# One pick in three beside attention added by VectorE, the first rotations moved into the projection's stage, and 64 candidate places for a head instead of 256

## The reference, cut to what matters

```python
sc = einsum('thpc,hpnc->thpn', q, sub_keys)            # 8 heads, 2 halves, 128 keys
v_half, i_half = lax.top_k(sc, 16)
cand = (v_half[:, :, 0, :, None] + v_half[:, :, 1, None, :]).reshape(t, 8, -1)   # 16 x 16
top_s, pos = lax.top_k(cand, 16)
expert = take_along_axis(cand_idx, pos, -1)            # 8 x 16 = 128 rows for a token
g = softmax(top_s)
act = gelu(einsum('thkd,td->thk', u_tab[expert], xc))
out = einsum('thk,thkd->td', g * act, v_tab[expert])
```

## Time and profile before

| | us |
|---|---|
| median of 3 runs | 2328.1 |
| the profiled execution: its own time | 2328.23 |
| its span | 2326.5 |
| PE busy | 1780.1 (77%) |
| DVE busy | 1429.7 (61%) |
| ACT busy | 786.7 (34%) |
| POOL busy | 625.0 (27%) |
| share of q0 (the gathers) in the DMA engines' time | 57.0% |
| chain that ended last: PE, DVE, DMA, ACT | 40%, 21%, 20%, 10% |

### The profile page before, as it was taken

One profiled execution on the slowest core, in us unless ns is written; L12 is line 12 of the kernel. 1 busy time (PEld: TensorE's weight loads), 2 busy tenths in 40 slices (PEclk: granted clock), 3 DMA queues, 4 the chain that ended last, 5 costly groups with the idle time before them and its releaser, 6 DMA issues.

```text
span 2326.5 us, 20848 instructions
## 1 busy us (share of the span) xinstructions
PE 1780.1 (77%) x6626; PEld 1047.3 (45%) x6626; DVE 1429.7 (61%) x2931; ACT 786.7 (34%) x2063; POOL 625.0 (27%) x524
## 2 busy tenths in 40 slices
PE   7587877757867875777787577664888989887987
PEld 3473333522323453332444423553333445566976
DVE  1448864698656479965637986658665234464644
ACT  1211453224334422432442234212564122433532
POOL 0001433444332333533234344425333000000000
PEclk9598989979998888998898898777899999888999
DMA  8068999999999899999989989999999655553542
GB/s 290 16 248 310 415 357 356 420 393 422 407 416 404 336 422 395 423 408 415 386 298 419 368 364 422 408 421 401 346 408 395 239 205 193 196 219 118 182 159 94
DMA packets 108828, 761.55 MB, mean 327 GB/s; under 512 B 13104, under 2 KB 14000, under 8 KB 18608
## 3 DMA queue, kind: packets, MB, share of 16 engines
q0 software_dynamic: 73728, 536.90, 57.0%
q1 hardware_dynamic: 32544, 215.45, 24.3%
q10 hardware_dynamic: 2448, 7.87, 0.9%
HBM read 759.12 MB, written 1.05 MB: 327 GB/s over the span
## 4 chain that ended last, share of the span: by engine, by line
PE 40%; DVE 21%; DMA 20%; ACT 10%; issue 6%; DVEq 1%; POOLq 1%; PEldq 1%; POOL 0%; ACTq 0%; PEld 0%; SPq 0%
DMA sb_work<-in_peer_uv,sb_expert 17%; PE ps_acc L1313 13%; PE bank L439 4%; DVE sb_work L1277 4%; PE bank L1143 3%; DVE sb_x L1285 3%; PE bank L1765 2%; DMA sb_wring<-in_peer_w_q 2%; PE bank L500 2%; PE bank L687 2%; PE ps_acc L1686 2%; ACT L1293 1%; PE bank L502 1%; PE bank L501 1%; ACT sb_probs L740 1%
## 5 line engine op out<-in xcount | busy, mean ns | idle before, releaser
L1313 PE MATMUL ps_acc<-sb_work,sb_diag 128*128 128x512 f32 x1500 | 774.3, 664 | 295.7 <-ACT sb_diag L1302 253.3
L2124 POOL DMA_INDIRECT sb_work<-in_peer_uv,sb_expert x512 | 622.6, 1216 | 1162.1 <-PE ps_acc L1313 587.9
L1277 DVE CUSTOM_DVE_ANT_0 sb_work<-sb_work,sb_h 128x1024 f32<-128x1024 f32 x512 | 620.3, 1223 | 283.7 <-DMA sb_work<-in_peer_uv,sb_expert 267.5
L1313 PEld LDWEIGHTS ps_acc<-sb_work,sb_diag 128*128 128x128 f32 x1500 | 299.7, 211 | 717.8 <-issue 701.0
L1293 ACT ACTIVATE sb_dots<-sb_dots 128x1 f32<-128x1 f32 x512 | 101.7, 199 | 470.7 <-DVE sb_dots L1277 440.8
L1285 DVE SCALAR_TENSOR_TENSOR sb_x<-sb_work,sb_weight,sb_x 128x1024 f32<-128x1024 f32 x137 | 175.5, 1281 | 51.3 <-ACT sb_weight L1294 51.3
L494 DVE TENSOR_TENSOR sb_work_r<-sb_wring,sb_work_r 128x2048 fp32r<-128x2048 f32 (+1 forms) x52 | 109.9, 2126 | 115.2 <-ACT sb_work_r L487 115.2
L439 PE MATMUL bank<-sb_wring,sb_hT 128*128 128x512 f32 (+2 forms) x392 | 158.1, 563 | 24.2 <-DVEq L280 17.4
L1302 ACT ACTIVATE sb_diag<-sb_ident,sb_weight 128x128 f32<-128x128 f32 x375 | 150.6, 401 | 33.0 <-PE ps_acc L1313 21.3
L1294 ACT ACTIVATE sb_weight<-sb_dots,sb_share 128x1 f32<-128x1 f32 x512 | 150.8, 294 | 16.6
L1143 PE MATMUL bank<-sb_hT,sb_wring 128*128 128x128 f32 x1024 | 124.7, 286 | 25.4 <-DMA sb_wring<-in_peer_w_q 22.6
(11 more groups left out here) (294 smaller groups left out, 2125.5 us busy)
## 6 DMA issues: line engine op xcount, KB each, us to landing
sb_wring<-in_w_mix SPq DMA_DIRECT2D x36, 1024.0 KB
sb_wring<-in_peer_w_q SPq DMA_DIRECT2D x32, 1024.0 KB
sb_wring<-in_w_gate SPq DMA_DIRECT2D x32, 1024.0 KB
sb_wring<-in_hyb_w_in SPq DMA_DIRECT2D x20, 1024.0 KB
sb_wring<-in_w_up SPq DMA_DIRECT2D x16, 1024.0 KB
sb_wring<-in_w_down SPq DMA_DIRECT2D x16, 1024.0 KB
sb_wring<-in_mla_w_uq SPq DMA_DIRECT2D x12, 768.0 KB
sb_wring<-in_hyb_w_out SPq DMA_DIRECT2D x8, 1024.0 KB
```

The source lines that it names most:

```text
L1277: e.tensor_tensor_reduce(u, u, h[:, t, :], 1.0, 0.0, ALU.mult, ALU.add, dots[:, i:i + 1]).then_inc(dot_ready, 1)
L1313: last = e.matmul(ps_acc[:, b * 512:(b + 1) * 512], diag[:, number % DIAGS, :], ring[:, n % RING, D + b * 512:D + (b + 1) * 512], start=k ...
L2124: pool.indirect_dma_start(ring[:, n % RING, :], None, a["peer_uv"], bass.IndirectOffsetOnAxis(ap=expert[:, t, n % P:n % P + 1], axis=0)).t ...
```

## The change

There are three edits.

1. The points of `attend` are marked `"both"`, and `share_out` gives a pick that falls on such a point to DVE if its number leaves 2 when divided by 3, and to PE otherwise. So 187 picks are added by DVE, where 137 were.
2. For tile 0, the eight rotations on DVE move from their own stage into the stage of the input projection. Before each, DVE waits until ACT has emptied the last block of columns that the rotation reads.
3. A head's second `top16` runs over 64 places instead of 256. They hold the pairs (row i, column j) of rows 0, 1 to 3, 4 to 7 and 8 to 15 with 16, 8, 4 and 1 columns, among which the 16 largest sums must be. Four smaller additions fill them, and ten more instructions of 128 elements turn a place back into row and column. The weights of the routing's points become smaller (71.5 to 56.5 us in all), so a little more of the picks falls on every other point of the first three feeds.

```diff
-                plan.append(g | value | {"points": [point(6.0), point(6.0)]})
+                plan.append(g | value | {"points": [point(6.0, "both"), point(6.0, "both")]})
...
-            dve_stage(steps)
+            if t:
+                dve_stage(steps)
+            else:
+                project_pe, project_act, _, emptied = project_parts(hT, a["hyb_w_in"], DC, EVEN_COLS, empty_even, "act",
+                                                                    tiles, first)
+                def rotate_behind(e):
+                    first["dve"](e)
+                    e.wait_ge(from_act.sem, sin_v)
+                    for col, rotate_heads in zip((VA, VA, VA, IK, IW, IW, KB, VB), steps):
+                        emptied(e, col)
+                        rotate_heads(e)
+                stage(pe=project_pe, act=project_act, dve=rotate_behind)
...
-            ranked = [point(us) for us in [9.0] + 5 * [6.5] + [3.0] + 6 * [4.5]]
+            ranked = [point(us) for us in [6.0] + 5 * [3.5] + [6.0] + 6 * [4.5]]
...
-                link(e.tensor_tensor(cand, b4[:, :, 0, :].unsqueeze(3).to_broadcast([P, EH, TOP, TOP]),
-                                     b4[:, :, 1, :].unsqueeze(2).to_broadcast([P, EH, TOP, TOP]), ALU.add))
+                for at, i0, ni, nj in ((0, 0, 1, 16), (16, 1, 3, 8), (40, 4, 4, 4), (56, 8, 8, 1)):
+                    link.add(e.tensor_tensor(
...
-                link.add(e.tensor_scalar(pick[0].bitcast(I32), at, 4, None, ALU.arith_shift_right))
-                link(e.tensor_scalar(pick[1].bitcast(I32), at, 15, None, ALU.bitwise_and))
...
+                link(e.tensor_scalar(hi, eighth, -1.0, 0.0, ALU.add, ALU.max))
+                link(e.scalar_tensor_tensor(hi, quarter, -6.0, hi, ALU.add, ALU.max))
+                link(e.scalar_tensor_tensor(hi, place, -48.0, hi, ALU.add, ALU.max))
...
+                link(e.tensor_tensor(lo, place, lo, ALU.subtract))
...
-                    if at is not None and f["filled"][at] == "pe":
+                    filled = None if at is None else f["filled"][at]
+                    if filled == "pe" or filled == "both" and k % 3 == 2:
```

More of the change, by code:

```diff
@@ L403, in project @@
         def project(xT, w, chunks, cols, empty, engine, tiles=range(TILES), first=None):
-            pe, other, points = project_parts(xT, w, chunks, cols, empty, engine, tiles, first)
-            both = {engine: other}
-            if first:
-                both["dve"] = first["dve"]
-            stage(pe=pe, points=points, **both)
+            pe, other, points, _ = project_parts(xT, w, chunks, cols, empty, engine, tiles, first)
+            stage(pe=pe, points=points, **{engine: other})
         def project_parts(xT, w, chunks, cols, empty, engine, tiles, first=None):
@@ L454, in other, with emptied @@
                     p(engine, e)
-            return pe, other, points
+            def emptied(e, col):
+                units = next(units for _, _, bn, c0, units, _ in plan if c0 + bn >= col)
+                units[-1].wait_emptied(e)
+            return pe, other, points, emptied
         places = [work_r[:, 2 * SLOT * i:2 * SLOT * (i + 1)] for i in range(4)] + [work_r[:, 0:SLOT], work_r[:, 3 * SLOT:4 * SLOT]]
@@ L1003, in enter_hybrid @@
             units = [turns.take() for _ in range(2)]
-            project_pe, project_act, _ = project_parts(hT, a["hyb_w_in"], DC, EVEN_COLS, empty_even, "act", [1])
+            project_pe, project_act, _, _ = project_parts(hT, a["hyb_w_in"], DC, EVEN_COLS, empty_even, "act", [1])
             def dve(e):
@@ L1035, in hybrid @@
                 turn_wide(H, hT, DC, tiles)
-                project(hT, a["hyb_w_in"], DC, EVEN_COLS, empty_even, "act", tiles, first)
             steps = []
@@ L1088, in build @@
         pick = [beside[:, 1280:1408], beside[:, 1408:1536]]
+        place, eighth, quarter = (beside[:, 1536 + i * P:1536 + (i + 1) * P] for i in range(3))
         iota16 = sb("iota16", [P, TOP])
@@ L1217, in dve @@
                 rest.pop(0)("dve", e)
[L1219 removed]
+                cf = key_scores.rearrange("p n k -> p (n k)")[:, 0:EH * 64].rearrange("p (h m) -> p h m", h=EH)
                 b4 = best.rearrange("p (h s) k -> p h s k", s=2)
[L1221 to L1222 removed]
@@ L1223, in dve @@
-                cf = key_scores.rearrange("p n k -> p (n k)").rearrange("p (h m) -> p h m", h=EH)
+                for at, i0, ni, nj in ((0, 0, 1, 16), (16, 1, 3, 8), (40, 4, 4, 4), (56, 8, 8, 1)):
+                    link.add(e.tensor_tensor(
+                        cf[:, :, at:at + ni * nj].rearrange("p h (i j) -> p h i j", i=ni),
+                        b4[:, :, 0, i0:i0 + ni].unsqueeze(3).to_broadcast([P, EH, ni, nj]),
+                        b4[:, :, 1, 0:nj].unsqueeze(2).to_broadcast([P, EH, ni, nj]), ALU.add))
@@ L1224, in dve @@
+                link.wait()
                 top16([(cf[:, j, :], top[:, j, :], top_at[:, j, :].bitcast(U32)) for j in range(EH)], [rest.pop(0) for _ in range(5)])
                 at = top_at.rearrange("p n k -> p (n k)").bitcast(I32)
-                link.add(e.tensor_scalar(pick[0].bitcast(I32), at, 4, None, ALU.arith_shift_right))
-                link(e.tensor_scalar(pick[1].bitcast(I32), at, 15, None, ALU.bitwise_and))
-                link.add(e.tensor_copy(hi, pick[0].bitcast(I32)))
-                link(e.tensor_copy(lo, pick[1].bitcast(I32)))
+                link.add(e.tensor_scalar(pick[0].bitcast(I32), at, 3, None, ALU.arith_shift_right))
@@ new lines, in dve @@
+                link.add(e.tensor_scalar(pick[1].bitcast(I32), at, 2, None, ALU.arith_shift_right))
+                link(e.tensor_copy(place, at))
+                link.add(e.tensor_copy(eighth, pick[0].bitcast(I32)))
+                link(e.tensor_copy(quarter, pick[1].bitcast(I32)))
+                link(e.tensor_scalar(hi, eighth, -1.0, 0.0, ALU.add, ALU.max))
+                link(e.scalar_tensor_tensor(hi, quarter, -6.0, hi, ALU.add, ALU.max))
+                link(e.scalar_tensor_tensor(hi, place, -48.0, hi, ALU.add, ALU.max))
@@ L1230, in dve @@
+                link.add(e.tensor_scalar(eighth, hi, 8.0, 8.0, ALU.mult, ALU.add))
+                link(e.tensor_scalar(quarter, hi, 4.0, 24.0, ALU.mult, ALU.add))
+                link(e.scalar_tensor_tensor(lo, hi, 16.0, eighth, ALU.mult, ALU.min))
+                link(e.scalar_tensor_tensor(quarter, hi, 48.0, quarter, ALU.add, ALU.min))
+                link(e.tensor_tensor(lo, lo, quarter, ALU.min))
+                link(e.tensor_tensor(lo, place, lo, ALU.subtract))
                 rest.pop(0)("dve", e)
```

1 line of the change is left out of this document (removed).

## The result

The changed kernel takes 2277.35 us (median of five runs, 2264.04 to 2280.89) where the kernel before takes 2333.31 (five runs). The ratio is 0.9759, 95% interval 0.9727 to 0.9791: 56 us less, between 49 and 64. The forecast was 2282, 46 less than the 2328.1 of then.

The account below looks back on a forecast made before the run. It took stage order as the bound early, then the queues' 421 GB/s ceiling, with attention falling short as POOL waited for PE's picks. Terms 12 + 4 + 5 + 25 = 46 us less than 2328.23 gave 2282 us, range 2254 to 2310.

Parts of the forecast that it names:

- Edit 2 (12 us): Stages before the first gather: tile 0's rotations end with the projection, PE starts transposes at 53.8 instead of 66.04, 12 us less.
- The small extra that the bounds allowed: Behind tile 0's rotations: up to 14 us less instead of 12 if PE, pausing less, keeps its clock.
- The first routing (4 us): First routing: DVE needs 6.4 us less, gathers could start that much earlier; between 2.3 and 6.4, 4 us was taken.
- The lower bound, by bytes: First routing: if bytes decide at once, only (421 - 356)/421 of 15 us comes back, 2.3 us.
- Attention (25 us): Both blocks' attention: two of six picks leave PE, slow groups fall from 19.6 to 16.8 us; 25 us less, bounds 0 to 45.
- the second block's, counted with 4: Second block's attention: its groups were partly at the queues' ceiling already, so 4 of 15.8 us lacking were counted.
- Attention fills to the ceiling: Rival, 20 in 100: attention's queues reach their ceiling, 70 us less in all, 2258 us.
- The clock: PE in attention: with fewer picks a second pick per group may run at 1.2 GHz, costing at most 34 us.
- rival of a cold PE: Rival, 7 in 100: the second cold pick costs 34 us against 28 of relief in attention; 2316 us, about no change.
- They lack 21/421 x 72 = 3.6 us there ... can bring at most these 10.5 us: Three later routings: shorter DVE part and fewer picks bring at most the queues' shortfall, 10.5 us; 5 us was taken.
- 4 + 5 us for edit 3: Routing's choice and point weights: 4 us less at the first routing, 5 us less in the three others together.
- The queues' floor of a group: Attention group: six gathers at 421 GB/s plus 0.35 pick more need 15.4 us, 0.7 us below the new PE loop.

## Why the prediction was right, and where it was not

The forecast of 46 us less was 10 short of the measured 56, and inside its range. That the absolute times lie closer (2282 and 2277) is luck: the kernel before took 5 us more in the later runs.

**Edit 2 (12 us)** held. PE's transposes start 12.3 us earlier, and alone it brought 10 us (6 to 14). The small extra that the bounds allowed, a clock that holds, is in the rows: the lead grows by 1.4 us between the transposes and the scores.

**The first routing (4 us)**: the forecast sum on DVE was 6.4 us, it measured 6.6, and the first gather came 7.6 us earlier with the places alone. Of that, 2.3 us were left at the end of attention 1. The lower bound, by bytes, was 2.3 as well; to the tenth that is chance, and in the whole nothing was left. The trace had said it: where the queues are nearly full, an early start is only worth the bytes that it adds. Taking 4, between the two bounds, was too much.

**Attention (25 us)** was right as a term. The additions alone bring 23 us (17 to 29), and what attention lacks in bytes falls by 23.6. The group went from 19.6 to 17.1, the forecast was 16.8. From its first copy to its last, the three attentions of the first block take 138.1 us in the changed kernel instead of 162.0, 24 less, with 24 counted. The shares are less exact: the second block's, counted with 4, gave 11.2 in the traces. PE's wait for the diagonal did not grow from 3.5 to 5 us but fell to 2.89. With every pick on DVE its loop is 18.0 us and it bounds; at one in three the loops are close enough that one in two brings no more than some 10 us. "Attention fills to the ceiling" did not come: 35.3 us of 71.5 are still lacking.

**The clock.** The rival of a cold PE did not come. In the group's window PE's clock is 0.90 of full, with 0.91 before. Over the whole attentions it fell a little: from 0.89, 0.86, 0.91 and 0.90 to 0.86, 0.88, 0.85 and 0.86. Beside picks the half clock lasted for whole windows only with every pick on DVE, where PE had next to nothing to add, and there PE was no longer the bound. The Trainium skill, "TensorE: Matmul & The Clock Gate", section "HAM oscillation — how this bites in real kernels", has it that waits between short bursts of matmuls bring the half clock back each time. The windows with 0.50 agree with that, and the pick of 2.94 us behind the wait of 2.89 points the same way. But the gain in attention did not shrink by most of itself: PE is slow behind its wait in the group after as it was in the group before.

**The step that was mis-sized** is "They lack 21/421 x 72 = 3.6 us there ... can bring at most these 10.5 us" (three times 3.6 is 10.8), from which 5 us were taken. Two things were left out. First, it looked at windows of 72 us. The stretches between the attentions are 183 to 205 us long and lack 31.0 us in all, of which the change brought 11. Second, and more, it named the "fewer picks there" but priced them by the routing's shortfall alone. The new weights move eleven picks out of the routings, and edit 1 makes room for them in attention, so that attention's lack falls by 36 us in the whole, where the additions alone bring 23.6 and the whole with the old weights 25.4. The runs show both halves: moved without room the picks cost 15 us, left in the routing with all else changed some 9, and the additions are worth 36 us with the new weights and places and 23 without. With 4 + 5 us for edit 3 the forecast had 9; against the two edits alone (-10 and -23) the whole has 23 more. Those 14 us, less 2 each for the other two edits, are the 10 between 46 and 56.

So edit 3 did not come out near its forecast when measured alone: its places (priced at 4 + part of 5) were worth nothing, its weights cost 15 us, and only in the whole are they worth some 11 and 9. Which share of the 23 us is whose, the runs do not say, as it depends on the order in which the parts are put in. That the sum landed within 10 us owes something to luck, because this interplay was not one of its terms.

Smaller slips did not decide anything. The queues' floor of a group, six rows and 0.35 more at 2.5 us, is 15.8 us and not 15.4. In the rival of a cold PE, 34 us against 28 of relief leave 6 and not 9. And the clock of 0.83 is not in the earlier trace rows, whose windows of attention show 0.89 to 1.00.

## What to carry to other kernels

Where the bound changes from stage to stage and a planner spreads work over them, price an edit by what it lets the planner move, not by the shortfall of its own stage alone. One pick moved out of the routing saved 1.3 us and cost 1.6 before attention had room, and saved 2.3 and cost 0.8 after. Where the bytes are fixed, add up what each stage lacks to the ceiling: a stage that gets shorter because its bytes have left it has gained nothing yet. Measure parts both alone and taken from the whole; here four parts sum to -18 us alone and make -56 together. And balance: the share of an engine that relieves another ends where its own loop meets the others', here somewhere between one in three and all, with one in two the best of the three by its median.

## What was not expected of the hardware

That independent DVE instructions follow each other faster than one lasts was used in the prediction; that it holds down to 64 elements was new. In the kernel after, maxima over 64 elements last 0.21 us each and start 0.13 us apart; four independent sums of 64 to 192 elements take 0.90 us together. So eight small ones in a row cost little, and it is the chain of dependent ones, 0.25 to 0.33 us for each of 128 elements, that made up most of the 3.5 us of the turning back.

With every pick on DVE, PE is granted 0.50 of its clock for windows of 55 and 90 us, and in the kernel before its six transposes after a pause of 13.1 us took 1.51 us, against 0.87 after one of 0.46 in the changed kernel.
